# A plain gate slab and the summed slab behind it, with TensorE's products interleaved

## The reference

```
def _swiglu(h, w_gu, w_down):
    gate, up = jnp.split(h @ w_gu, 2, axis=-1)
    return (jax.nn.silu(gate) * up) @ w_down

x = x + 0.5 * _swiglu(_rmsnorm(x, ffn1_norm[l]), ffn1_w_gu[l], ffn1_w_down[l])
```

## Time and profile before

| | |
|---|---|
| median of three runs | 3015.25 us (3014.38 to 3019.18) |
| the profiled execution's own time | 3015.76 us |
| its span, first to last instruction | 3013.9 us |
| TensorE busy (PE), weight loads (PEld) | 2993.6 us (99%), 2672.2 us (89%) |
| VectorE (DVE), GpSimd (POOL), ScalarE (ACT) busy | 2139.0 us (71%), 1532.1 us (51%), 1501.6 us (50%) |
| TensorE's mean granted clock | 0.998 |

### The profile page before, as it was taken

The page is one execution under the profiler, slowest core; times in us unless marked ns, Lnnn a source line. Parts: engine busy times, 40 slices in busy tenths (PEclk is TensorE's granted clock), DMA queues, the critical chain, the costliest instruction groups (busy, mean ns, idle before and its releaser), DMA issues.

```text
span 3013.9 us, 48048 instructions
## 1 busy us (share of the span) xinstructions
PE 2993.6 (99%) x19120; PEld 2672.2 (89%) x19120; DVE 2139.0 (71%) x3446; ACT 1501.6 (50%) x1999; POOL 1532.1 (51%) x749
## 2 busy tenths in 40 slices
PE   9999999999999999999999999999999999999998
PEld 7888888888999999998888888888899998999997
DVE  4899886764324457787688887777579866789764
ACT  6555544444667455544555554444544454544454
POOL 5787764445565555585677875444550004710013
PEclk9999999999999999999999999999999999999999
DMA  6888877885776554465688788787576446665455
GB/s 219 285 275 277 277 276 249 306 286 185 225 176 178 158 166 150 148 172 199 206 281 283 268 282 281 245 304 271 178 214 196 155 147 216 181 191 180 154 182 181
DMA packets 491671, 663.43 MB, mean 220 GB/s; under 512 B 70440, under 2 KB 278040, under 8 KB 490936
## 3 DMA queue, kind: packets, MB, share of 16 engines
q1 hardware_dynamic: 485960, 655.85, 66.5%
q0 software_dynamic: 4448, 2.94, 0.3%
q10 hardware_dynamic: 1040, 1.58, 0.2%
HBM read 656.06 MB, written 2.11 MB: 218 GB/s over the span
## 4 chain that ended last, share of the span: by engine, by line
PE 95%; DVE 3%; ACT 1%; DMA 0%; issue 0%; POOL 0%; DVEq 0%; ACTq 0%
PE ps L1138 33%; PE ps L1002 20%; PE ps L1143 17%; PE ps L1008 10%; PE ps L1019 3%; PE ps L1171 2%; PE ps L1024 1%; PE ps L1167 1%; PE ps L986 1%; DVE narrow_split_slabs L2254 1%; PE ps L1660 1%; PE ps L1177 1%; PE ps L1439 1%; PE ps L1420 1%; PE ps L1174 1%; PE ps L1109 0%
## 5 line engine op out<-in xcount | busy, mean ns | idle before, releaser
L921 POOL TENSOR_TENSOR split_slabs<-stage,split_slabs 128x1024 fp32r<-128x1024 f32 x366 | 892.4, 2448 | 1008.3 <-ACT split_slabs L1716 1001.8
L1716 ACT ACTIVATE split_slabs<-stage 128x1024 fp32r<-128x1024 f32 x544 | 572.8, 1059 | 550.6 <-PE ps L1143 438.9
L1716 ACT ACTIVATE narrow_split_slabs<-stage 128x1024 fp32r<-128x1024 f32 (+1 forms) x437 | 457.4, 1051 | 607.1 <-PE ps L1008 458.6
L1138 PE MATMUL ps<-split_slabs,h_split 128*128 128x512 f32 x2904 | 719.7, 390 | 0.8 <-ACT split_slabs L1716 0.8
L1138 PEld LDWEIGHTS ps<-split_slabs,h_split 128*128 128x128 f32 x2904 | 541.7, 188 | 111.4 <-ACT split_slabs L1716 1.2
L1002 PE MATMUL ps<-h_split,narrow_split_slabs 128*128 128x256 f32 x4928 | 621.9, 279 | 2.4 <-issue 1.9
L921 POOL TENSOR_TENSOR narrow_split_slabs<-stage,narrow_split_slabs 128x1024 fp32r<-128x1024 f32 (+1 forms) x182 | 441.5, 2436 | 315.0 <-ACT narrow_split_slabs L1716 314.6
L1002 PEld LDWEIGHTS ps<-h_split,narrow_split_slabs 128*128 128x128 f32 x4928 | 587.4, 188 | 13.8 <-issue 8.7
L2254 DVE TENSOR_TENSOR split_slabs<-stage,split_slabs 128x1024 fp32r<-128x1024 f32 x178 | 255.8, 1439 | 273.2 <-ACT split_slabs L1716 272.3
L2254 DVE TENSOR_TENSOR narrow_split_slabs<-stage,narrow_split_slabs 128x1024 fp32r<-128x1024 f32 x255 | 340.2, 1337 | 124.4 <-ACT narrow_split_slabs L1716 123.2
L1143 PE MATMUL ps<-split_slabs,h_split 128*128 128x512 f32 x1452 | 388.2, 389 | 0.0
(11 more groups left out here) (346 smaller groups left out, 3295.6 us busy)
## 6 DMA issues: line engine op xcount, KB each, us to landing
stage<-in_ffn_w_gu SPq DMA_DIRECT2D x352, 512.0 KB, 4.7
stage<-in_w_in SPq DMA_DIRECT2D x349, 512.0 KB, 3.5
U<-in_w_ada SPq DMA_DIRECT2D x192, 512.0 KB, 5.4
stage<-in_ffn_w_down SPq DMA_DIRECT2D x176, 512.0 KB, 5.1
stage<-in_w_out SPq DMA_DIRECT2D x96, 512.0 KB, 4.2
stage<-in_w_in SPq DMA_DIRECT2D x80, 128.0 KB, 2.9
stage<-in_w_branch_c SPq DMA_DIRECT2D x32, 192.0 KB, 3.4
stage<-in_cmp_w SPq DMA_DIRECT2D x8, 512.0 KB, 4.7
```

The costliest lines, as they stand in the source:

```text
L921: nc.gpsimd.tensor_tensor(slab_part(n, 1, size(n)), stage[:, n % RING, 0:size(n)], slab_part(n, 0, size(n)).bitcast(F32), ALU.subtract).th ...
L1138: mm(ps[:, 2 * pair + T, :], stationary(kk, i)[:, T * P:(T + 1) * P], w[0][:, kk, :], start=first and kk == 0 and i == 0, stop=False)
L1716: return fn(slab_part(n, 0, size(n)), stage[:, n % RING, 0:size(n)], ACT.Copy)
```

## The change

`summed_passes` becomes `paired_passes`. It is called for the plain slab n (q = 2, 4, 6) and does that slab and the summed slab n + 1 together; at q = 3, 5, 7 the loop then does nothing more. The matmuls are the same 33, with the same operands and sums, in another order:

- wait for the high part of n; then eight wide matmuls of it, with one narrow matmul of the plain high part of n + 1 behind each of the first six (the wait for `plain_hi` stands ahead of the first narrow one);
- wait for the low part of n; then four wide matmuls of it, with two narrow ones of the sums' high part behind each (the wait for that part stands ahead of the first of these; slab n is counted in `slab_done` by the fourth wide one);
- the three and the four narrow matmuls of the low parts as before.

The wait for the combined tokens stands ahead of the first pair. Nothing else in the program differs.

```
-                pe.wait_ge(plain_hi, nth_sum[n])
-                for k, (stationary, sums_to) in enumerate(of_plain):
-                    for i in range(2):
-                        mm(sums_to, stationary(i), whole[0][:, k, :], start=first and k == 0 and i == 0, stop=False)
                 pe.wait_ge(hi_done, nth[n])
-                for k, (stationary, sums_to) in enumerate(of_sums):
-                    for i in range(2):
-                        mm(sums_to, stationary(i), sums[0][:, k, :], start=first and k == 0 and i == 0, stop=False)
-                pe.wait_ge(plain_lo, nth_sum[n])
+                for kk in range(WK):
+                    for T in range(TT):
+                        for i in range(2):
+                            wide(kk, T, i, 0)
+                            k = 2 * kk + T
+                            if (k, i) == (0, 0):
+                                pe.wait_ge(plain_hi, nth_sum[n + 1])
+                            if k < 3:
+                                of_plain_hi(k, i)
+                pe.wait_ge(*slab_split(n))
+                for kk in range(WK):
+                    for T in range(TT):
+                        ins = wide(kk, T, 0, 1)
+                        k = 2 * kk + T
+                        if k == 0:
+                            pe.wait_ge(hi_done, nth[n + 1])
+                        if k == 3:
+                            ins.then_inc(slab_done, 1)
+                        for i in range(2):
+                            of_sums_hi(k, i)
+                pe.wait_ge(plain_lo, nth_sum[n + 1])
...
                             if n in nth_sum:
-                                if (j, q) == (STR_GROUPS[0], STR_SLABS[0]):
+                                between(n - s0)
+                                continue
+                            if n + 1 in nth_sum:
+                                if (j, q + 1) == (STR_GROUPS[0], STR_SLABS[0]):
                                     pe.wait_ge(comb_ready, f + 1)
-                                summed_passes(gate_acc(f), n, q, q == STR_SLABS[0], q == 7)
+                                paired_passes(gate_acc(f), n, q, q + 1 == STR_SLABS[0], q == 6)
                                 between(n - s0)
                                 continue
```

More of the change, by code:

```diff
@@ L1145, in wide_passes, with paired_passes, wide @@
                 ins.then_inc(slab_done, 1)
[L1147 to L1152, removed]
+            def paired_passes(pair, n, q, first, last):
+                m = STR_SLABS.index(q + 1)
+                w = [slab_part(n, i).rearrange("p (c w) -> p c w", c=WK) for i in range(2)]
+                whole = [col_blocks(plain_part(n + 1, i)) for i in range(2)]
+                sums = [col_blocks(slab_part(n + 1, i)) for i in range(2)]
                 def tokens(kk, T):
-                    return lambda i: hx[:, i, WK * q + kk, T * P:(T + 1) * P]
+                    return lambda i: hx[:, i, WK * (q + 1) + kk, T * P:(T + 1) * P]
                 def combined(s):
                     return lambda i: comb[:, i, s, m * P:(m + 1) * P]
+                def wide(kk, T, i, which):
+                    return mm(ps[:, 2 * pair + T, :], hx[:, i, WK * q + kk, T * P:(T + 1) * P], w[which][:, kk, :], start=False, stop=False)
                 low, high = slice(0, STR_COLS), slice(STR_COLS, WN)
@@ L1172, in summed_passes, with of_plain_hi, of_sums_hi @@
-                pe.wait_ge(plain_lo, nth_sum[n])
+                def of_plain_hi(k, i):
+                    stationary, sums_to = of_plain[k]
+                    mm(sums_to, stationary(i), whole[0][:, k, :], start=first and k == 0 and i == 0, stop=False)
+                def of_sums_hi(k, i):
+                    stationary, sums_to = of_sums[k]
+                    mm(sums_to, stationary(i), sums[0][:, k, :], start=first and k == 0 and i == 0, stop=False)
+                pe.wait_ge(hi_done, nth[n])
@@ L1173, in summed_passes @@
+                pe.wait_ge(plain_lo, nth_sum[n + 1])
                 for k, (stationary, sums_to) in enumerate(of_plain):
                     mm(sums_to, stationary(0), whole[1][:, k, :], start=False, stop=last and k == 2)
-                pe.wait_ge(*slab_split(n))
+                pe.wait_ge(*slab_split(n + 1))
                 for k, (stationary, sums_to) in enumerate(of_sums):
```

## The result

The changed kernel took 3022.6 us (median of 17 runs, 3019.45 to 3025.88) against 3016.0 us for the kernel before in the same comparison (17 runs, 3014.38 to 3020.83): a ratio of 1.002, 95% interval 1.0013 to 1.0026, so 3.9 to 7.8 us slower. The forecast of 3016 and its range, which ended at 3020, missed it. The same two kernels were timed against each other twice more: 1.0007 (0.9998 to 1.0016) and 0.9998 (0.9989 to 1.0007). What the change costs and why three comparisons of the same pair differ are two questions, and the traces answer them apart.

The account below looks back on a forecast made before the run. The prediction took TensorE's matmul spacing as the bound: pair terms 2.78 + 1.17 + 0.48 + 0.84 + 0.01 = 5.28 us against 5.26, 48 x 0.02 = +1.0 us on 3015.25, said as 3016. Range 3010.5 to 3020 us.

Parts of the forecast that it names:

- What bounds the kernel: Whole kernel: TensorE holds 95% of the chain, busy 99%; the change can move only how closely matmuls follow each other.
- The waits: Earlier needs and later slab release: 3.9 and 1.5 us to spare; some ScalarE waits up to 1.4 us later, covered.
- The narrow products: 21 per pair: ten directly behind wide ones 1.17 us, four second behind 0.48 us, closing seven 0.84 us.
- The wide products: Twelve per pair: ten at 0.232 us, two at 0.229 us, 2.78 us together.
- rows 6: Profile rows of wide products behind a narrow run, before the change: starts 70.55 to 71.71, 0.232 us each for five.
- the slower rival: All 48 pairs: wide products at 0.235 us, narrow at 0.12; +4.3 us, 3019.6, or +7.2 us, 3022.5; chance 0.10.
- alternation never settles: The slower rival: 5.35 us a pair, or 5.41 with wide products at 0.24; chance 0.10.
- What would show it: Profile after: one wide and one narrow 0.345 to 0.352 us, pair 5.22 to 5.34 us, closing seven at 0.12, no idle.
- The terms named for the lower end: Pair's range 5.22 to 5.34 us: lower end from direct narrow products at 0.113 and wide ones at 0.229.
- the mean of the wide ones at which 6 us are reached: Slower rival: decides above a mean of 0.239 us for wide products, where 0.2%, 6 us, is passed.
- The rival by which the order is without effect: Gate pairs: loads still start one product ahead, unsettled 0.03 us stays; change 0, 3015.2 us; chance 0.18.
- How the numbers follow: Whole time: +1.0 us put on the median 3015.25 gives 3016.2, said as 3016; gates' own range 3013.3 to 3019.

Follow-up runs that it names:

- the added transposes: A wait and a 128 x 128 transpose ahead of pieces of the long narrow runs, in both kernels: 3024.29 us without the change, 3026.64 us with it.

## Why the prediction was wrong

- *What bounds the kernel: right.* TensorE, by the distance of its matmuls. No wait was added.
- *The waits: right.* ScalarE's idle time that TensorE ends (line waited in, released by, us in total, times, longest) was 438.9 us, in

```profile
ACT split_slabs L1716 <- PE ps L1143: 438.9, 292, 2.0
```

and is 403.4 + 46.3 = 449.7 us, 0.7 us a group more, where under 1.5 was said:

```profile
ACT split_slabs L1745 <- PE ps L1143: 403.4, 269, 2.0
...
ACT split_slabs L1745 <- PE ps L1162: 46.3, 32, 3.2
```

- *The narrow products: right.* Directly behind a wide one 0.1172 us (0.117 said), second 0.119 (0.12), the closing seven 0.1192 each, 0.83 together (0.84).
- *The wide products: the term that failed.* "I take 0.232 for the ten that never have five wide products to settle, the mean of the five in rows 6", 2.78 us for twelve. Measured 12 x 0.2348 = 2.82 us; this term alone carries the gates' miss, 1.3 us. The mean of five consecutive wide products behind a narrow run was taken for wide products that each stand behind a narrow one. The right row was beside it: the first two behind a run, 0.235, the value of the slower rival. With it the sum is 2.82 + 1.17 + 0.48 + 0.83 + 0.01 = 5.31 against 5.26, +0.05 us a pair, +2.4 us. So the narrow terms of the forecast and the wide term of its rival "alternation never settles" were true together; the rival's 0.12 for every narrow product was not.
- *What would show it.* One wide and one narrow at 0.353 us lie just past the 0.352 set as the bound of the forecast and under the rival's 0.355; the pair, 5.30, lies within 5.22 to 5.34. (The terms named for the lower end give 5.21, and the mean of the wide ones at which 6 us are reached is 0.238, not 0.239; nothing hangs on either.)
- *The rival by which the order is without effect: fell.* With the same products in another order each of the 16 groups takes 0.146 us more, in all four traces of the changed kernel. The Trainium skill ("TensorE: Matmul & The Clock Gate", section "Back-to-back issue gap") also says that in a stream of loads and products the spacing is set by both, pipelined through a reorder window. The trace agrees so far as a wide product takes 0.2265 or 0.2348 us by what stands beside it; no run here parts the load from the product or shows the window.
- *How the numbers follow: the second failure, and the larger in us.* The time missed by 6.4 us, of which the wide term is 1.3: with it right, the forecast would have been 3017.6. The time was put on a median of three runs, 3015.25, and the range was made from the gates' terms alone, so that the scatter from execution to execution stood in it at nothing. The earlier trace rows show two spacings of the same 256-column products. The forecast used them for the gates and did not ask what they are worth in the long runs: 720 products x 0.0045 us = 3.2 us for one draw, more than the whole change. The kernel before had medians of 3016.0, 3017.28, 3019.23 and 3020.79 us in four comparisons. A true cost of 2.4 us with such a base would have been 3018 to 3023 by itself.

What stays open: the first comparison shows 3.7 us beyond the gates' 2.3. The one execution of it that has a trace, the fastest of the seventeen, lost 3.2 - 0.7 us in the long runs, but the other sixteen have none; that they drew the slow spacing more often than the kernel before did is a guess that no trace shows. The other traces do not favour it: of the 22 long runs in the eleven traces without the added transposes five are slow, and of the eight of the changed kernel one. Draws made anew in each execution would also average out over 17 runs on each side, to within 1.4 us. Something that lasts through a whole comparison was not tested; the second and the third ran on different chips.

Nor are the long runs the only draw. Between the two traces of the kernel before, the start alone differs by 1.1 us, and a narrow stage from 905 us on by 1.1 us, at 0.113 us in one and 0.118 in the other. In five of the thirteen traces TensorE's granted clock falls at 845 us from 1.00 to 0.50 (from 2.4 to 1.2 GHz), behind the same sixteen products of 30 columns as in those where it stays, and all that follows comes 1.5 us later. The stretch in the kernel before (first fence) and in the second trace of the changed one (second; busy us and counts by engine, PE first, then the granted clock, which is the third number from the end):

```profile
845.00:848.40 3.40, 3.40 (x30) 3.40 (x30) 2.13 (x1) 0.27 (x1) 1.05 (x1) 1.00 0.91 188
```

```profile
845.00:848.40 3.40, 3.40 (x18) 3.40 (x17) 1.83 (x1) 0.00 (x0) 0.75 (x1) 0.50 0.99 209
```

Why a run of narrow products draws one spacing or another is open, but in the narrow stages it goes with the step by which the run is entered. Among the runs of at least 20 products in all thirteen traces, counted from 700 us on, those that start 220 to 223 ns after the narrow product ahead of them go on at 0.113 us in 478 of 500 cases, and those that start 225 to 227 ns after it at 0.118 us in 152 of 156. What sets that step no run shows. Why the runs of the gates always take the slowest spacing is open too.

## What to carry to other kernels

Where TensorE is the bound as here, price a reordering by the place of each product behind its neighbour, not by a mean over a run that settles: keep products of one size together, or at least in twos, and do not alternate singles. Look in the trace for long runs of equal products that stand at another spacing at another time, multiply the difference by their number, and put that into the range before anything else. Where a change is worth less than that draw, count its own stage in the trace, and make the other stages alike in both kernels before timing.

## What the runs showed of the hardware that was not expected

- Singles of 512 and 256 columns in alternation take 0.353 us a pair in a cycle of three; in twos a group takes 21.220 us as in the order of before, since late wide products and faster narrow ones cancel, and in alternation of equal sizes all is settled at 0.2265 us.
- A long run of 256-column products stands at 0.113 or 0.118 us through some 720 products, unless a wait breaks it, and the choice differs between executions of the same program; of the 14 pieces behind an added wait and transpose 13 stood at 0.118, the same 13 in both kernels.
- A restart 220 to 223 ns behind the last narrow product is followed by 0.113 us in 478 of 500 runs, one of 225 to 227 ns by 0.118 us in 152 of 156.
- The granted clock falls from 1.00 to 0.50 at 845 us in some executions and not in others, between the same instructions, at a cost of 1.5 us.
